# One more projection step behind the triangular inverse's second level, one fewer at the end of each head

## What is computed

```python
proj = h @ w_in
qkv = silu(short_conv(proj[..., OFF_Q:OFF_G], conv_w))
...
lmat = where(strict, einsum(k_beta, k) * decay, 0.0)
a = lmat + eye(CHUNK)
sol = triangular_solve(a, rhs, lower=True, unit_diagonal=True)
...
v_new = u_c - w_c @ S
o_c = q_c @ S + attn_c @ v_new
S = S * d_c + k_c^T @ v_new
...
o = o * rsqrt(mean(o * o) + EPS) * onorm_g * silu(gate)
```

## Time and profile before

| | us |
|---|---|
| median of 3 runs | 2383.14 |
| lowest and highest | 2380.79, 2383.86 |
| the profiled execution, its own time | 2380.56 |
| its span, first to last instruction | 2378.8 |
| the eight heads, head 0's first matmul to the last transpose of head 7 | about 113 to 1182 of the span |

### The profile page before, as it was taken

The page is one execution under the profiler, slowest core; times in us unless marked ns, Lnnn a source line. Parts: engine busy times, 40 slices in busy tenths (PEclk is TensorE's granted clock), DMA queues, the critical chain, the costliest instruction groups (busy, mean ns, idle before and its releaser), DMA issues.

```text
span 2378.8 us, 39734 instructions
## 1 busy us (share of the span) xinstructions
PE 2297.4 (97%) x14208; PEld 1681.5 (71%) x14208; DVE 1110.7 (47%) x2161; ACT 928.5 (39%) x2437; POOL 372.8 (16%) x270
## 2 busy tenths in 40 slices
PE   6999999999999999999999999779999999999997
PEld 3456666665756666665644444579999999999997
DVE  3587787868686877766336317710010000100003
ACT  4173746465563747465321133213222232222323
POOL 2040413122230404132100000000011100011101
PEclk9999999999999999999999999889999999999999
DMA  9710212120201202121442322368868888688885
GB/s 351 257 42 21 70 38 70 38 70 18 90 18 42 66 20 70 29 70 41 174 166 90 136 89 98 143 229 293 289 232 279 285 292 294 239 267 285 292 292 211
DMA packets 198882, 362.31 MB, mean 152 GB/s; under 512 B 9082, under 2 KB 72519, under 8 KB 195723
## 3 DMA queue, kind: packets, MB, share of 16 engines
q1 hardware_dynamic: 191994, 341.73, 41.2%
q0 software_dynamic: 6528, 19.47, 3.2%
q10 hardware_dynamic: 273, 0.11, 0.0%
HBM read 320.63 MB, written 40.65 MB: 152 GB/s over the span
## 4 chain that ended last, share of the span: by engine, by line
PE 91%; DVE 4%; DMA 2%; issue 1%; ACT 1%; SPq 0%; DVEq 0%; POOLq 0%; POOL 0%; ACTq 0%
PE bank L823 23%; PE bank L2537 21%; PE bank L2551 11%; PE bank L2150 5%; PE bank L1887 5%; PE bank L809 3%; PE bank L1031 2%; PE bank L801 2%; PE bank L1905 2%; PE bank L1023 2%; PE bank L1089 2%; PE bank L1100 1%; PE bank L1105 1%; PE bank L1016 1%; PE bank L1104 1%
## 5 line engine op out<-in xcount | busy, mean ns | idle before, releaser
L823 PE MATMUL bank<-arena 128*128 128x512 f32 x1344 | 679.5, 607 | 0.9
L2537 PE MATMUL bank<-arena 128*128 128x144 f32 x4096 | 512.6, 286 | 3.1 <-ACT arena L2571 3.1
L2537 PEld LDWEIGHTS bank<-arena 128*128 128x128 f32 x4096 | 509.3, 190 | 3.2 <-ACT arena L2571 3.2
L2644 DVE TENSOR_TENSOR arena<-arena,bank 128x144 f32<-128x144 f32 x128 | 39.1, 306 | 697.4 <-ACT arena L2585 697.4
L823 PEld LDWEIGHTS bank<-arena 128*128 128x128 f32 x1344 | 215.7, 191 | 87.9 <-issue 86.5
L2551 PE MATMUL bank<-arena 128*128 128x144 f32 x2048 | 257.3, 286 | 0.7 <-DVE arena L2644 0.7
L2551 PEld LDWEIGHTS bank<-arena 128*128 128x128 f32 x2048 | 253.8, 189 | 1.9 <-DVE arena L2644 0.9
L2585 ACT ACTIVATE arena<-bank 128x144 f32<-128x144 f32 x128 | 37.5, 293 | 460.5 <-PE bank L2537 460.5
L1031 PEld LDWEIGHTS bank<-arena 128*128 128x128 f16 x1296 | 97.1, 98 | 157.9 <-issue 139.8
L1209 ACT ACTIVATE arena<-bank 128x384 f16<-128x384 f16 (+1 forms) x360 | 159.7, 493 | 105.7 <-PE bank L1031 94.5
L1294 DVE SCALAR_TENSOR_TENSOR arena<-arena 128x1156 f32<-128x1156 f32 x96 | 150.1, 1563 | 1.3
(11 more groups left out here) (327 smaller groups left out, 3071.3 us busy)
## 6 DMA issues: line engine op xcount, KB each, us to landing
arena<-in_exp_w_gate SPq DMA_DIRECT2D x32, 2048.0 KB, 10.2
arena<-in_exp_w_up SPq DMA_DIRECT2D x32, 2048.0 KB, 15.1
arena<-in_exp_w_down SPq DMA_DIRECT2D x32, 2048.0 KB, 10.8
arena<-in_w_in SPq DMA_DIRECT2D x52, 512.0 KB, 5.4
arena<-in_ada_w SPq DMA_DIRECT2D x24, 1024.0 KB, 8.1
side_dram<-arena SPq DMA_DIRECT2D x20, 576.0 KB, 4.2
arena<-g_dram SPq DMA_DIRECT2D x16, 576.0 KB, 4.2
arena<-in_x_sample SPq DMA_DIRECT2D x16, 512.0 KB, 5.8
```

Of the source, the lines that this page charges most:

```text
L823: ins = nc.tensor.matmul(bank[:, 0:LH], w[:, k, :], x[:, k, :], start=(k == 0 and job[2] in "127"), stop=(k == KH - 1), skip_group_check=( ...
L2537: last = nc.tensor.matmul(banks[3 + f % 2][:, m * CAP:(m + 1) * CAP], w_unit[2 * half + m][:, k, col:col + P], xsT[:, k, :], start=(k == 0 ...
```

## The change

One condition in the table of steps. Before, the places `P4_2` and `P8_2`, those of the last product of the second and of the third level, had no side step; now only `P8_2` has none.

```diff
-        FILL |= {f"{x}{b}_{g}": 0 if b in LEVELS[1:3] and (x, g) == ("P", 2) else 2 if (x, b, g) == ("P", 64, 2) else 1 for b in LEVELS for x in "ZP" for g in range(3)}
+        FILL |= {f"{x}{b}_{g}": 0 if b == LEVELS[2] and (x, g) == ("P", 2) else 2 if (x, b, g) == ("P", 64, 2) else 1 for b in LEVELS for x in "ZP" for g in range(3)}
```

## The result

| | before | after |
|---|---|---|
| median of 8 runs, us | 2382.44 | 2390.57 |
| lowest and highest | 2380.79, 2384.70 | 2389.53, 2392.65 |
| profiled execution, its own time | 2380.56 | 2392.65 |
| its span | 2378.8 | 2390.9 |
| a head of the loop (heads 1 to 5), first matmul to the next head's first | 131.33 | 132.49 |

The changed kernel takes 1.0037 times as long, with a 95% interval of 1.0029 to 1.0046. That is 8.1 us between the medians; the forecast was 8.2, and 2391.3 for the time (the median of before was 2383.14 when it was made, 0.7 more than that of the eight runs here).

What follows compares the result with a forecast made beforehand. PE, busy for 97% of the span, was taken as the bound. Seven loop heads at +1.19 us and the last head gave +8.2 on the median of 2383.14, so 2391.3 us; the forecast's own range was 2388 to 2394.

Steps and rivals of the forecast that it cites:

- the new step at P4_2: Level 4's last product: the added side step costs PE 0.91 us in a head.
- waits at Z8_0 and Z8_1: Before level 8's first two transposes: the new step covers PE's waits of 0.23 and 0.14 us, -0.37 a head.
- qv4's sum ahead of level 8: On DVE: qv4's addition now precedes `join(0)` and makes it late, +0.30 us a head, bounds 0 and 0.68.
- `fix`: Eight side matmuls in `fix`: kg5 is added earlier, so kg3's first step stops waiting, -0.42 us a head.
- the scan and the rest: Small steps and sums moved within the scan: taken as 0, bounded by 0.24 us a head either way.
- the boundary: Head's end to next head's start: AB4's sum delays the reduction and AB3's copy, +0.77 us, bounds -0.5 and +0.9.
- the last head: Final head: new step and waits +0.91 - 0.37, AB4's sum at level 16 +0.21, one step less 0.86; total -0.11 us.
- Rivals 1 and 2: Reduction not held at the boundary: 1, level 8 also free, 2380.1 or 2377.6, 9%; 2, level 8 costs, 2382.4, 5%.
- Rival 3: Only the boundary costs, `join(0)` at level 8 not late: 0.89 us a head, 2389.2 us; chance 9%.
- rival 4: Level 8 and scan delays at their upper bounds, +0.68 and +0.24: 1.81 us a head, 2395.7 us; chance 7%.

## Why the prediction came out

By its own steps, for a head of the loop:

| step | forecast | measured |
|---|---|---|
| the new step at P4_2 | +0.91 | +0.91 |
| waits at Z8_0 and Z8_1 | -0.37 | -0.39 |
| qv4's sum ahead of level 8 | +0.30 | +0.31 |
| `fix` | -0.42 | -0.40 |
| the scan and the rest | 0 | +0.03 |
| the boundary | +0.77 | +0.70 |
| a head of the loop | +1.19 | +1.16 |
| the last head | -0.11 | +0.35 |

**The new step** and its waits came as worked out, and the swapped step shows why the waits go: DVE's chain, not PE's order, sets when they end.

**qv4's sum** was rightly priced, and its cause holds by the experiment that moved it. The latency from the last matmul's start to the addition, taken from AB5 at 0.63, served at this place too: the last matmul of qv4, PE, starts 0.63 ahead of the addition at 558.93.

```profile
558.30 0.59 PE L823 MATMUL bank<-arena 128*128 128x512 f32 x1
```

**`fix`** holds by the experiment that did it alone.

**The scan** was taken at nothing, and it came to almost nothing because its parts cancel: the wait ahead of `correct(3)` went and one of 0.38 came in `predict(3)`, behind its first product, and `advance` changed by 0.08 at three places, twice up and once down. No run here does that part alone; its size is read from the traces only.

**The boundary** rests on two experiments, one that takes the sum away (-1.25) and one that adds it alone (+1.55). The forecast was 0.07 too high: it had the reduction 1.3 late, which came 1.27 late, and it let AB3's copy start near the listed end of the SiLU, 1.26 behind its start, where the copy starts 1.17 behind it (645.97 to 647.14).

**The last head** was mis-sized: +0.35 where the sum had -0.11. Of the terms that it had, the waits at level 8 came to -0.39 and the delay of AB4's sum at level 16 to +0.22, for +0.21. The step less at its end gave 0.86, as worked out. What failed is that its sum has no term for the scan, which I had weighed for the loop heads alone. The one place more by which the list is ahead leaves one small step where there were more, and `correct(5)` waits. The last head's tile 5, PE, before and then after:

```profile
1147.23 1.06 PE L809 MATMUL bank<-arena 128*128 128x128 f32 x8
1148.12 0.61 PE L1089 MATMUL bank<-arena 128*128 128x128 f32 x4
```

```profile
1157.51 0.39 PE L809 MATMUL bank<-arena 128*128 128x128 f32 x2
1157.89 0.75 PE L1089 MATMUL bank<-arena 128*128 128x128 f32 x4
```

Eight of the small matmuls take 1148.12 - 1147.23 = 0.89, so two take 0.22, and the products of `correct` start 0.38 behind the first of them: they wait for their operand. Around this place the last head lost 0.29, with 0.10 more at its start and 0.07 at the transposes behind level 64. That is read from the traces; no run moves those small steps alone, but the run with AB4's sum behind the reduction has the same last head, 146.19 for 146.18, so it isn't AB4's sum at the boundary.

**The sum.** Heads 1 to 5 make 5 x 1.16 = 5.80, head 6 1.02, the last 0.35, head 0 only 0.71, together 7.9; the forecast was 8.2. Head 0 is not like the others: it takes 135.22 in the kernel before, not the 131.3 that I gave for all seven, and it pays 0.45 less. Of this, 0.25 stands ahead of P4_2, where the change has done nothing yet. In the first 17 us of head 0 the granted clock was 0.90 in the profiled executions of the changed kernel and of three runs (qv4's sum behind level 8, AB4's sum ahead, the step swapped), and 1.00 in those of the kernel before and of the other three. The four at 0.90 reach the first product of L1016, 18 us into the head, 0.20 to 0.41 sooner than the kernel before, the others 0.03 to 0.04 sooner. So this part goes with the execution and not with the change. In the changed kernel DVE's nine instructions of L1351 take 5.49 us there instead of 6.52, with four of POOL's additions (L1303) beside them instead of five; that this is the cause, no run here shows. Of the rest, 0.17 is a wait in the scan's tile 2 that head 0 of the kernel before has and the other heads don't. The two misses, of head 0 and of the last head, have opposite signs and nearly cancel, so that the sum comes within 0.3 of the forecast is in part luck; the terms of heads 1 to 6 are not.

**The rivals.** Rivals 1 and 2 needed the reduction to stay released by POOL; in the trace after it follows L871. The run with the sum behind the reduction is what they described for the boundary, -0.55. Rival 3 needed `join(0)` not to be late, rival 4 a whole addition; the 0.31 lies between. Near rival 1 the prediction had also put the result if a closed gap is a gain, which it took as the aim of the Trainium skill's page "Perfetto Trace Analysis", section "Optimization Strategy". Here the gap closed and the head got longer. What the page asks for, dependencies that start sooner or complete faster, moving a step doesn't do; the run with POOL's sum later did it, and won.

## What to carry to other kernels

Moving a step by one place in a fixed list can move the consumers that are tied to the list, and the cost is set by what stands, in the consumer's engine's program, behind the one that now waits: here one addition of 0.69 us, placed ahead of the head's last chain, cost 1.25 us a head, more than the step. Before filling a gap of the busiest engine, ask whose chain ends it; where that chain had no slack of its own, filling the gap won nothing (1.0000), and shortening it did (0.47 us a head). The price of such a wait could be read ahead here from another place with the same pair of instructions, start to start (0.63 us at both).

## What the runs showed of the hardware

I had not looked for POOL's addition holding up DVE. A copy of L1409, which reads its mask and its data from SBUF, took 1.53 us beside POOL's L1303 against 0.56 without it, and it ended at 542.11, 0.42 behind POOL's end at 541.69. The Trainium skill, page "SBUF — State Buffer", section "Who interferes with whom", says that a DVE instruction with two SBUF inputs contends with a GpSimd instruction that reads SBUF, and that the lock is exclusive. The trace agrees, as far as it goes: moving L1303 out of the way brought the 0.56 back. The same stands at level 16 of head 3 in the kernel before, beside another POOL instruction:

```profile
561.08 0.80 DVE L1409 COPY_PREDICATED arena<-arena 128x384 f16<-128x384 uint32 x1
```

```profile
558.83 2.63 POOL L1581 TENSOR_TENSOR arena<-arena 128x1152 f32<-128x1152 f32 x1 [4.28 <-DVE arena L1414]
```

This copy too ends (561.88) 0.42 behind POOL's end (561.46). DVE instructions that read one of their inputs from PSUM weren't held up: `join` (L1402) beside the same L1581, at 560.37, took its usual 0.56, and the addition of L871 beside POOL's 2.23 us the same 0.68 as elsewhere. The prediction had weighed POOL for the addition only; the changed kernel has both slow copies as well (1.52 and 0.79 us), so they are no part of the difference.
